# Output projections of a two-block network: modulation folds before additions, norm sums on TensorE alone, a rescale spread over a projection's tiles

## The chip, the cores and the metric

The kernel runs on one core of one Trainium2 chip. The metric is device time in microseconds for one execution of the whole program. Engines are named as the profile names them: PE is TensorE's matmuls and PEld its weight loads, DVE is VectorE, ACT is ScalarE, POOL is GpSimd, SP is SyncE, which issues the DMAs.

## The reference, cut to what matters

Two networks run one after the other on a sequence of 512 tokens with 1024 features. The first has two layers; each ends in an output projection that is added to `x`, and then `x` is normalised. The second opens with a norm whose gain and shift ("modulation") come from a vector `c` times a large weight matrix.

```python
# first block, per layer
h = rms_norm(x, norm_g[layer])
p = h @ w_in[layer]                       # first and second projection
...                                       # attention of two kinds, gated
x = x + mixed @ w_out[layer]              # the output projection "out1"
# after both layers
x = rms_norm(x, final_g)

# second block, per layer l
mod = silu(c) @ ada_w[l, i] + ada_b[l, i] # shift, scale, gate: 3 x 1024 values
h = _rmsnorm(x, norm_g[l, 0]) * (1.0 + scale) + shift
p = h @ ab_w_in[j]                        # the third projection, "pab"
...
x = x + gate * mix
```

All operands are fp32. Products of weights and activations are made in three passes with operands split in a high and a low part: high times high, high times low, low times high.

## The kernel before, in words

Everything is kept transposed: features on the 128 partitions, the 512 tokens along the free axis. `x` is eight tiles (`m.x[:, k]`, KD = 8) of 128 x 512. A "stage" is a block of code for all engines with its own semaphores, closed by a barrier of all engines (L68). Within a stage each engine has its own program in a fixed order written out by hand, and waits for others by semaphore counts; an instruction behind a waiting one on the same engine waits too.

**The output projection of the first block** (`project_out`, stage "out1", once for each layer, so twice) goes over eight output tiles t. For each, SP loads a weight tile of 512 KB into a ring of four slots (`first` and three of `out_raw`), ACT rounds it to its high part (`upper`, L320), DVE makes the low part (`lower`, L327), PE runs 3 x 8 products of 128 x 512 into bank t % 4 (`products_by_half`, L352, L356, L359), and DVE adds the bank to `x` (L1132). Tile t + 4 waits for that addition. `pair`, which holds high and low parts, has two slots. Tile 0's high and low parts of the activations (L1105, L1121) are made beside its products.

Beside it, for the norm of the next stage, `TokenSums` sums the squares of `x` over the features. With a weight it has two chains: squares of x, and squares of x times the gain `final1`. ACT makes both squares of a tile (L138, L140) into two slots `out_sq`. POOL folds them (L150): tiles 1 to 6 are added to an accumulator per chain. At the end PE sums columns (L155): for a chain of 512 tokens it takes four matmuls with 128 x 128 weights and a moving operand of one column of ones, first of the accumulator, then of the last square. Since fp32 matmuls are recorded as two passes, four matmuls show as 8 rows; a tile of both chains is 16 rows. `straight` is the other way of `TokenSums`, used in the opening stage: no accumulator, PE sums the columns of each square, and the slot is free when PE has read it (`freed`); L136 waits for it.

Also beside it, `Modulations` makes one third of a layer's modulation: `c` times a weight matrix that comes in eight chunks of 1024 KB through a ring of four (`ada_ring`, SP, L510). A chunk n of 4 or more waits until chunk n - 4 is folded. DVE folds a pair of chunks in two halves, k = 0 to 3 and 4 to 7 (L528, L531: eight instructions of 128 x 256 a half), with one half in each tile, after the addition of the tile before. `ada_acc` holds two pairs, so pair 2 waits for PE's sum of pair 0, and pair 3 for that of pair 1. PE sums the columns of a pair with four one-column matmuls (L541, 8 rows). `keep` (L549) copies the result out, L1144 and L1146 finish it, and `invert` (L185) turns the root of the token sums into its reciprocal.

SP's order of loads in out1: weights 1 and 2, modulation chunks 0 and 1, weight 3, chunks 2 and 3, weights 4 and 5, chunks 4 and 5, weights 6 and 7, chunks 6 and 7, then the first tile of the next stage's weights.

**The third projection** (`project`, stage "pab", once, behind the second out1) has 35 tiles of 24 products and then four token tiles. It begins with a norm: DVE spreads the reciprocals (L228), PE stretches them over the partitions (L234), DVE and ACT scale, shift, round and split eight tiles (L274, L260, L262, L278) while PE runs the products of tiles 0 and 1 tile by tile of `x` (`first_products`, L292). `TwoNorms` does two norms in one, so `x` itself must still be multiplied by the first norm's gain: `replace` (L1533, eight instructions on `x`), which needs its own `spread.widen` on DVE (L228) and `spread.stretch` on PE (L234, bank 6). It stands on DVE between the norm and the loop over tiles, followed by `bounds.differences` (five tiny operations, L1480 to L1483) and `beside.begin` (L2558, L2559). Then comes the loop: `lower` of tile 2 and so on. `pair` has two slots here, so `upper` of tile 2 waits for the products of tile 0.

Of the kernel before, what the change touches and what calls it, by code (L numbers as in the profile page):

```python
# [28 lines left out]
KD = D // P  # L29
# [41 lines left out]
class Count:  # L71
# [13 lines left out]
    def step(self, ins):  # L85
        self.done(ins)
        self.wait()
# [30 lines left out]
class TokenSums:  # L118
# [34 lines left out]
    def columns(self, pe, what, n, first, last):  # L153
# [3 lines left out]
                                       skip_group_check=True)  # L157
        return mm

    def sum(self, pe):  # L160

        if self.straight:
            for k in range(KD):
                pe.wait_ge(self.squared, k + 1)
                mm = self.columns(pe, self.sq[:, k % 2, 0], 0, k == 0, k == KD - 1)
                mm.then_inc(self.freed if k < KD - 1 else self.summed, 1)
            return
        pe.wait_ge(self.freed, self.chains * (KD - 2))
        for n in range(self.chains):
            self.columns(pe, self.acc[:, n], n, n == 0, False)  # L170
        for n in range(self.chains):
            pe.wait_ge(self.squared, self.chains * (KD - 1) + n + 1)
            mm = self.columns(pe, self.sq[:, (KD - 1) % 2, n], n, False, n == self.chains - 1)
        mm.then_inc(self.summed, 1)
# [872 lines left out]
def project_out(nc, m, name, w, kt, src, gate, follow, down=None, layer=None):  # L1047
# [4 lines left out]
    with stage(nc, name) as sem, ExitStack() as c:  # L1052
# [5 lines left out]
        made, added, rounded, split = sem("made"), sem("added"), sem("rounded"), sem("split")  # L1058
        high, low = sem("high"), sem("low")
        ada = None if layer is None else Modulations(nc, m, c, sem, layer, 2, m.ps[:, 6])  # L1060
        sums = TokenSums(nc, m, c, sem, name, False, None if layer is None else param(m, "final1"))
        following = sem("following")

        with nc.Block(no_gpsimd_drain=True) as block:
            @block.sync
            def _(sp):

                for t in range(KD):
                    ring.load(sp, split, w, t + 1, first=t)
                    if ada is not None and t in (2, 3, 5, 7):  # L1070
                        ada.load(sp, {2: range(2), 3: range(2, 4), 5: range(4, 6), 7: range(6, 8)}[t])

                if follow is not None:
                    if whole:
                        sp.wait_ge(split, 5)
                    sp.dma_start(m.first[:], follow).then_inc(following, 16)
                    sp.wait_ge(following, 16)

            @block.tensor
            def _(pe):  # L1080
                def part(b, k):
                    return parts[:, b, k]

                for t in range(KD):
                    if t >= 4:
                        pe.wait_ge(added, t - 3)
                    first = t == 0 and whole
                    products_by_half(nc, pe, m.ps[:, t % 4], lambda a, k: pair[:, t % 2, a, k], part, kt, t, rounded,
                                     split, high if first else None, low if first else None).then_inc(made, 1)
                    if ada is not None and t in (4, 6):  # L1090
                        ada.sum(pe, t // 2 - 2)
                sums.sum(pe)
                if ada is not None:
                    ada.sum(pe, 2)
                    ada.sum(pe, 3)

            @block.gpsimd
            def _(pool):
                sums.fold(pool)

            @block.scalar
            def _(act):
# [14 lines left out]
            def _(dve):  # L1117
# [7 lines left out]
                for t in range(KD + 1):  # L1125
                    if 1 <= t < KD:
                        lower(nc, dve, ring, pair, rounded, split, t)
                    if t >= 1:
                        j = t - 1
                        dve.wait_ge(made, j + 1)  # L1130
                        if gate is None:
                            ins = nc.vector.tensor_tensor(m.x[:, j], m.ps[:, j % 4], m.x[:, j], ALU.add)  # L1132
                        else:
                            ins = nc.vector.scalar_tensor_tensor(m.x[:, j], m.ps[:, j % 4], gate[:, j:j + 1],  # L1134
                                                                 m.x[:, j], ALU.mult, ALU.add)
                        ins.then_inc(added, 1)
                    if ada is not None and t >= 1:
                        first = (t - 1) % 2 * (KD // 2)
                        ada.fold(dve, (t - 1) // 2, range(first, first + KD // 2))
                if ada is not None:  # L1140
                    ada.keep(dve)
                    flat = m.modf[:].rearrange("p i n -> p (i n)")
# [186 lines left out]
def param(m, name, k=0, n=None):  # L1329
    return param_columns(m.params, name, k, n)  # L1330


def project(nc, m, name, w, norm, places, token_places=(), beside=None, edges=(), tables=(), slots=3, two=None, bounds=None):
# [4 lines left out]
    with stage(nc, name) as sem, ExitStack() as c:  # L1338
# [15 lines left out]
        with nc.Block(no_gpsimd_drain=True) as block:  # L1354
# [13 lines left out]
            @block.tensor  # L1368
            def _(pe):
                def turn(n):  # L1370
                    pe.wait_ge(taken, tiles + n + 1)
                    if n >= 2:
                        pe.wait_ge(placed, n - 1)
                    for i in range(TT):
                        mm = nc.tensor.transpose(m.ps[:, 4 + n % 2, i * P:i * P + P],
                                                 flat[:, n % 2, i * P:i * P + P], m.ident[:])
                    mm.then_inc(turned, 1)

                norm.spread.stretch(pe)
                norm.first_products(pe, (m.ps[:, 0], m.ps[:, 1]), pair, split, made)  # L1380
                if two is not None:
                    two.spread.stretch(pe)
                for t in range(2, total):
                    pe.wait_ge(split, t + 1)
                    if t >= 4:
                        pe.wait_ge(taken, t - 3)
                    products(nc, m.ps[:, t % 4], lambda a, k: pair[:, t % slots, a, k],
                             lambda b, k: norm.to[:, b, k], kt).then_inc(made, 1)
                    if t > tiles:
                        turn(t - 1 - tiles)  # L1390
                if total > tiles:
                    turn(total - 1 - tiles)

            @block.scalar
            def _(act):
# [10 lines left out]
                for t in range(total + 2):  # L1406
                    if slots == 2 and 2 <= t < total:
                        upper(nc, act, ring, pair, rounded, made, t)
                    if bounds is not None and t == 6:
                        bounds.powers(act)  # L1410
                    if 1 <= t <= total:
                        j = t - 1
# [11 lines left out]
            def _(dve):  # L1424
                if two is not None:
                    two.inverse(dve)
                norm.scale(dve, lambda t: lower(nc, dve, ring, pair, rounded, split, t),
                           None if two is None else two.both)
                if two is not None:
                    two.replace(dve)  # L1430
                    bounds.differences(dve)
                dve.wait_ge(zeroed, len(edges))
                if beside is not None:
                    beside.begin(dve)
                for t in range(total):
                    if t >= 2:
                        lower(nc, dve, ring, pair, rounded, split, t)
                    if bounds is not None and t == 8:
                        bounds.values(dve)
                    if beside is not None and t >= 3:  # L1440
                        beside.step(dve, taken, t - 3)
# [54 lines left out]
class TwoNorms:  # L1496
# [28 lines left out]
        self.nc.scalar.activation(self.both[:], self.both[:], ACT.Sqrt, bias=self.m.eps[:, 0:1], scale=1.0 / D)\  # L1525
            .then_inc(self.rooted, 1)

    def replace(self, dve):
        nc, m = self.nc, self.m
        self.spread.widen(dve)  # L1530
        dve.wait_ge(self.spread.stretched, 1)
        for k in range(KD):
            nc.vector.scalar_tensor_tensor(m.x[:, k], m.x[:, k], param(m, "final1", k, 1), m.ps[:, 6],  # L1533
                                           ALU.mult, ALU.mult).then_inc(self.replaced, 1)


def chunk_ends(ap, d):
# [1595 lines left out]
```

## Time and profile before

| | us |
|---|---|
| runs of the kernel before | 2878.0, 2873.0, 2867.95 (median 2873.0) |
| the profiled execution's own time | 2864.47 |
| its span, first to last instruction | 2862.5 |
| PE busy in the span | 2561.8 (89%) |
| DVE / ACT / POOL busy | 1551.0 / 941.7 / 231.6 |
| mean granted TensorE clock | 0.939 of full |
| first out1 stage, first weight issue to L185 | 535.27 to 599.04 |
| second out1 stage, first weight issue to L185 | 1122.15 to 1186.04 |
| third projection, from | 1187.24 |

A row of the timeline reads: start, duration, engine, line, operation, tiles, shape, number of merged instructions, and in brackets how long the engine was idle before it and what ended that. Durations of merged rows reach from the first start to the last end. A granted clock of 1.00 is 2.4 GHz, 0.50 is 1.2 GHz.

### The profile page before, as it was taken

What the parts mean: (1) busy time and instruction counts of PE and PEld (TensorE: products, weight loads), DVE (VectorE), ACT (ScalarE), POOL (GpSimd) and SP (SyncE); (2) the same over time, 40 slices, a digit from 0 to 9 for tenths busy, and PEclk for the clock granted to TensorE, in tenths of its full rate; (3) what the DMA queues carried; (4) which work ended last, traced back from release to release, by engine and by line L of the source; (5) the groups of instructions that cost most, each with busy time, mean ns of one, the idle gap of its engine ahead of it and who ended that gap; (6) DMA issues with size and microseconds to landing.
All of it is one profiled execution on the core that took longest, in us unless ns stands there. A gap on an engine that the chain in (4) does not pass through costs nothing. (4 is left out here: it accounts for less than half of the span.)

```text
span 2862.5 us, 44705 instructions
## 1 busy us (share of the span) xinstructions
PE 2561.8 (89%) x19054; PEld 2062.6 (72%) x19092; DVE 1551.0 (54%) x2240; ACT 941.7 (33%) x1399; POOL 231.6 (8%) x208
## 2 busy tenths in 40 slices
PE   8999899989998999799676988689999896899998
PEld 7888675668886766678564877478878773788877
DVE  3474467863743668725446655654552397445522
ACT  4223124432231245332433333243332322433321
POOL 0000000110000000200152322000001100100011
PEclk9999999989999989799887999799999897999999
DMA  3222223322222133222110000223222121222231
GB/s 134 96 97 96 80 90 124 146 91 96 98 94 84 60 127 134 109 96 96 38 46 15 4 3 4 96 74 103 97 105 109 38 82 44 74 98 94 87 122 50
DMA packets 56106, 238.20 MB, mean 83 GB/s; under 512 B 6560, under 2 KB 7328, under 8 KB 47328
## 3 DMA queue, kind: packets, MB, share of 16 engines
q1 hardware_dynamic: 55904, 235.30, 23.5%
q8 instruction: 153, 2.51, 0.4%
q14 instruction: 49, 0.40, 0.0%
HBM read 231.08 MB, written 4.19 MB: 82 GB/s over the span
## 5 line engine op out<-in xcount | busy, mean ns | idle before, releaser
L341 PE MATMUL banks<-b_h,pin_pair 128*128 128x512 f32 x2304 | 528.3, 390 | 0.0
L341 PEld LDWEIGHTS banks<-b_h,pin_pair 128*128 128x128 f32 x2304 | 431.1, 188 | 88.9
L341 PE MATMUL banks<-ffh,ff_pair 128*128 128x512 f32 x2016 | 457.3, 389 | 0.0
L341 PEld LDWEIGHTS banks<-ffh,ff_pair 128*128 128x128 f32 x2016 | 378.4, 188 | 78.5
L341 PE MATMUL banks<-b_h,pab_pair 128*128 128x512 f32 x792 | 182.4, 392 | 8.0 <-DVE pab_pair L327 8.0
L341 PEld LDWEIGHTS banks<-b_h,pab_pair 128*128 128x128 f32 x792 | 149.9, 190 | 39.4 <-DVE pab_pair L327 8.2
L531 DVE SCALAR_TENSOR_TENSOR ada_acc<-ada_ring,sc,ada_acc 128x256 f32<-128x256 f32 x336 | 158.2, 538 | 0.0
L2680 DVE TENSOR_TENSOR ff<-ff_c,ff 128x512 fp32r<-128x512 f32 x44 | 30.5, 692 | 204.8 <-ACT ff L2668 203.4
L327 DVE TENSOR_TENSOR pin_pair<-pin_raw,pin_pair 128x1024 fp32r<-128x1024 f32 x50 | 61.3, 1226 | 140.1 <-ACT pin_pair L320 140.1
L1134 DVE SCALAR_TENSOR_TENSOR x<-banks,modf,x 128x512 f32<-128x512 f32 x32 | 24.0, 751 | 205.4 <-PE banks L359 205.4
L327 DVE TENSOR_TENSOR pin_pair<-first,pin_pair 128x1024 fp32r<-128x1024 f32 x50 | 61.3, 1226 | 125.3 <-ACT pin_pair L320 125.3
L320 ACT ACTIVATE ff_pair<-ff_raw 128x1024 fp32r<-128x1024 f32 x58 | 61.4, 1059 | 182.4 <-PE banks L341 182.4
L352 PE MATMUL banks<-ff,dn_pair 128*128 128x512 f32 x352 | 87.2, 405 | 13.8 <-ACT dn_pair L320 13.8
L2880 DVE SCALAR_TENSOR_TENSOR cd_acc<-b_hb,params,cd_acc 128x512 f32<-128x512 f32 x120 | 90.2, 752 | 4.0
L320 ACT ACTIVATE dn_pair<-dn_raw 128x2816 fp32r<-128x2816 f32 x16 | 40.9, 2557 | 152.7 <-PE banks L359 142.4
L352 PEld LDWEIGHTS banks<-ff,dn_pair 128*128 128x128 f32 x352 | 69.2, 197 | 29.5 <-ACT dn_pair L320 14.7
L750 ACT ACTIVATE dil_pt<-banks 128x1024 f32<-128x1024 f32 x32 | 32.8, 1025 | 163.1 <-PE banks L676 163.1
L2378 DVE COPY_PREDICATED ru_inv<-rw_levels,banks 128x512 f32<-128x512 uint32 (+1 forms) x80 | 53.7, 677 | 54.1 <-PE banks L2207 54.0
L356 PE MATMUL banks<-ff,dn_pair 128*128 128x512 f32 x352 | 82.4, 389 | 0.0
L359 PE MATMUL banks<-ff,dn_pair 128*128 128x512 f32 x352 | 82.4, 389 | 0.0
L359 PEld LDWEIGHTS banks<-ff,dn_pair 128*128 128x128 f32 x352 | 66.1, 188 | 13.7
L356 PEld LDWEIGHTS banks<-ff,dn_pair 128*128 128x128 f32 x352 | 66.1, 188 | 13.7
(514 smaller groups left out, 4489.9 us busy)
## 6 DMA issues: line engine op xcount, KB each, us to landing
ada_ring<-in_ada_w SPq DMA_DIRECT2D x48, 1024.0 KB, 7.9
ff_raw<-in_ffn_up SPq DMA_DIRECT2D x58, 512.0 KB, 3.7
pin_raw<-in_w_in SPq DMA_DIRECT2D x50, 512.0 KB, 3.5
first<-in_w_in SPq DMA_DIRECT2D x48, 512.0 KB, 3.5
dn_raw<-in_ffn_down SPq DMA_DIRECT2D x16, 1408.0 KB, 6.0
first<-in_ffn_up SPq DMA_DIRECT2D x30, 512.0 KB, 3.5
pab_raw<-in_ab_in SPq DMA_DIRECT2D x23, 512.0 KB, 3.5
out_raw<-in_w_out SPq DMA_DIRECT2D x12, 512.0 KB, 9.0
```

The lines of the kernel that those rows point to most:

```text
L320: nc.scalar.activation(pair[:, t % slots, 0], ring.at(t), ACT.Copy).then_inc(rounded, 1)
L327: nc.vector.tensor_tensor(pair[:, t % slots, 1], ring.at(t), pair[:, t % slots, 0].bitcast(F32), ALU.subtract).then_inc(split, 1)
L341: mm = nc.tensor.matmul(bank, w(a, k), x(b, k), start=k == 0 and i == 0, stop=k == kt - 1 and i == 2)
L352: nc.tensor.matmul(bank, w(0, k), x(0, k), start=k == 0, stop=False)
L356: nc.tensor.matmul(bank, w(0, k), x(1, k), start=False, stop=False)
L359: mm = nc.tensor.matmul(bank, w(1, k), x(0, k), start=False, stop=k == kt - 1)
L531: ins = nc.vector.scalar_tensor_tensor(acc, w, self.m.sc[:, k:k + 1], acc, ALU.mult, ALU.add)
L750: nc.scalar.activation(pt[:, s:s + 2], m.ps[:, s:s + 2], ACT.Exp, scale=scale)\
L1134: ins = nc.vector.scalar_tensor_tensor(m.x[:, j], m.ps[:, j % 4], gate[:, j:j + 1], m.x[:, j], ALU.mult, ALU.add)
L2378: nc.vector.copy_predicated(inv[:, i % 2, f:2, e], over(m.levels[:, d, l, f:2]), m.ps[:, 4 + e, 2 * f * P:].rearrange("p (k t n) -> p k t ...
L2680: chain.step(nc.vector.tensor_tensor(ff[:, 1, j], cv[:, j % 2], ff[:, 0, j].bitcast(F32), ALU.subtract))
L2880: ins = nc.vector.scalar_tensor_tensor(acc[:, k], hb[:, k, tap:tap + T], w[:, 4 * tap + k:4 * tap + k + 1], acc[:, k], ALU.mult, ALU.add)
```

## The change

In `project_out` with a layer (the two out1 stages): the modulation fold of a tile stands on DVE before the addition of the tile before, and one tile earlier (it starts at t = 0); the chunks are asked for earlier; PE sums a modulation pair after tiles 3, 5, 7 instead of 4 and 6 and the end; the token sums go the straight way, with `step` k after tile k + 3, the rest at the end; POOL does nothing. In `project` with two norms (the third projection): the second stretch stands behind tile 3 on PE, its widening in tile 2 on DVE, one of the eight rescales of `x` in each of tiles 6 to 13, `differences` in tile 5, `values` in tile 10 and not 8, and ACT's `powers` in tile 8 and not 6.

```diff
+    def step(self, pe, k):
+        for n in range(self.chains):
+            pe.wait_ge(self.squared, self.chains * k + n + 1)
+            mm = self.columns(pe, self.sq[:, k % 2, n], n, k == 0 and n == 0, k == KD - 1 and n == self.chains - 1)
+        mm.then_inc(self.freed if k < KD - 1 else self.summed, 1)
+
...
-        sums = TokenSums(nc, m, c, sem, name, False, None if layer is None else param(m, "final1"))
+        sums = TokenSums(nc, m, c, sem, name, layer is not None, None if layer is None else param(m, "final1"))
...
                 for t in range(KD):
                     ring.load(sp, split, w, t + 1, first=t)
-                    if ada is not None and t in (2, 3, 5, 7):
-                        ada.load(sp, {2: range(2), 3: range(2, 4), 5: range(4, 6), 7: range(6, 8)}[t])
+                    if ada is not None and t in (1, 2, 3, 5):
+                        n = (1, 2, 3, 5).index(t)
+                        ada.load(sp, range(2 * n, 2 * n + 2))
...
-                    if ada is not None and t in (4, 6):
-                        ada.sum(pe, t // 2 - 2)
-                sums.sum(pe)
-                if ada is not None:
-                    ada.sum(pe, 2)
+                    if ada is not None and t >= 3 and t % 2 == 1:
+                        ada.sum(pe, t // 2 - 1)
+                    if sums.straight and t >= 3:
+                        sums.step(pe, t - 3)
+                if sums.straight:
+                    sums.step(pe, KD - 3)
+                    sums.step(pe, KD - 2)
                     ada.sum(pe, 3)
+                    sums.step(pe, KD - 1)
+                else:
+                    sums.sum(pe)
...
-                sums.fold(pool)
+                if not sums.straight:
+                    sums.fold(pool)
...
                 for t in range(KD + 1):
                     if 1 <= t < KD:
                         lower(nc, dve, ring, pair, rounded, split, t)
+                    if ada is not None and t < KD:
+                        ada.fold(dve, t // 2, range(t % 2 * (KD // 2), t % 2 * (KD // 2) + KD // 2))
                     if t >= 1:
...
-                    if ada is not None and t >= 1:
-                        first = (t - 1) % 2 * (KD // 2)
-                        ada.fold(dve, (t - 1) // 2, range(first, first + KD // 2))
...
                 norm.first_products(pe, (m.ps[:, 0], m.ps[:, 1]), pair, split, made)
-                if two is not None:
-                    two.spread.stretch(pe)
...
+                    if two is not None and t == 3:
+                        two.spread.stretch(pe)
...
-                    if bounds is not None and t == 6:
+                    if bounds is not None and t == 8:
                         bounds.powers(act)
...
-                if two is not None:
-                    two.replace(dve)
-                    bounds.differences(dve)
...
-                    if bounds is not None and t == 8:
+                    if two is not None and t == 2:
+                        two.spread.widen(dve)
+                    if two is not None and 6 <= t < 6 + KD:
+                        two.replace(dve, t - 6)
+                    if bounds is not None and t == 5:
+                        bounds.differences(dve)
+                    if bounds is not None and t == 10:
                         bounds.values(dve)
...
-    def replace(self, dve):
+    def replace(self, dve, k):
         nc, m = self.nc, self.m
-        self.spread.widen(dve)
         dve.wait_ge(self.spread.stretched, 1)
-        for k in range(KD):
-            nc.vector.scalar_tensor_tensor(m.x[:, k], m.x[:, k], param(m, "final1", k, 1), m.ps[:, 6],
-                                           ALU.mult, ALU.mult).then_inc(self.replaced, 1)
+        nc.vector.scalar_tensor_tensor(m.x[:, k], m.x[:, k], param(m, "final1", k, 1), m.ps[:, 6],
+                                       ALU.mult, ALU.mult).then_inc(self.replaced, 1)
```

## Rows read from the trace of the kernel before

**Rows 1.** Page, part 1.

```profile
PE 2561.8 (89%) x19054; PEld 2062.6 (72%) x19092; DVE 1551.0 (54%) x2240; ACT 941.7 (33%) x1399; POOL 231.6 (8%) x208
```

**Rows 2.** Timeline of the first out1, tiles 4 to 7, all engines, cut.

```profile
564.88 5.30 DVE L531 SCALAR_TENSOR_TENSOR ada_acc<-ada_ring,sc,ada_acc 128x256 f32<-128x256 f32 x8
565.70 3.01 POOL L150 TENSOR_TENSOR out_acc<-out_acc,out_sq 128x512 f32<-128x512 f32 x2 [3.95 <-ACT out_sq L138]
566.70 0.95 PE L541 MATMUL banks<-ones,ada_acc 128*128 128x1 f32 x8
567.51 2.11 PE L352 MATMUL banks<-out_parts,out_pair 128*128 128x512 f32 x8
...
577.96 0.68 DVE L1132 TENSOR_TENSOR x<-banks,x 128x512 f32<-128x512 f32 x1
578.09 2.11 PE L359 MATMUL banks<-out_parts,out_pair 128*128 128x512 f32 x8 [0.97 <-DVE out_pair L327]
578.56 3.25 DVE L531 SCALAR_TENSOR_TENSOR ada_acc<-ada_ring,sc,ada_acc 128x256 f32<-128x256 f32 x8
```

**Rows 3.** Timeline of the first out1, its end; the second's is alike, 586.9 later.

```profile
584.62 1.97 PE L359 MATMUL banks<-out_parts,out_pair 128*128 128x512 f32 x8
588.15 2.48 PE L155 MATMUL banks<-ones,out_acc 128*128 128x1 f32 x16 [1.56 <-POOL out_acc L150]
591.28 3.58 PE L155 MATMUL banks<-ones,out_sq 128*128 128x1 f32 x16 [0.65 <-ACT out_sq L138]
...
599.04 0.17 DVE L185 RECIPROCAL rms<-rms 128x4 f32<-128x4 f32 x1
```

**Rows 4.** Stretches: length, PE, PEld, DVE, ACT, POOL busy, PEclk, DMA share, GB/s.

```profile
580.00:586.00 6.00, 6.00 (x32) 5.05 (x31) 6.00 (x10) 1.25 (x2) 6.00 (x3) 1.00 0.00 0
...
588.10:589.40 1.30, 1.25 (x11) 1.25 (x12) 1.30 (x4) 0.00 (x0) 0.00 (x0) 0.99 0.05 13
...
591.30:594.80 3.50, 3.50 (x17) 3.50 (x17) 2.43 (x7) 2.03 (x3) 0.00 (x0) 0.50 0.00 0
...
1877.50:1883.00 5.50, 3.02 (x25) 2.79 (x23) 1.80 (x6) 0.98 (x3) 0.14 (x2) 1.00 0.07 18
...
2846.80:2849.00 2.20, 1.48 (x14) 1.39 (x12) 0.75 (x1) 1.21 (x2) 0.00 (x0) 1.00 0.00 0
```

**Rows 5.** Timeline of the third projection, end of the norm to tile 3.

```profile
1210.91 1.05 PE L234 MATMUL banks<-ident,two_spread 128*128 128x128 f32 x8
1210.92 1.05 ACT L320 ACTIVATE pab_pair<-pab_raw 128x1024 fp32r<-128x1024 f32 x1
...
1218.67 1.23 DVE L327 TENSOR_TENSOR pab_pair<-pab_raw,pab_pair 128x1024 fp32r<-128x1024 f32 x1
...
1219.95 30.41 PE L341 MATMUL banks<-b_h,pab_pair 128*128 128x512 f32 x124 [7.99 <-DVE pab_pair L327]
...
1227.73 0.60 ACT L1417 ACTIVATE hq<-banks 128x512 f32<-128x512 f32 x1 [14.33 <-PE banks L341]
...
1233.17 0.60 ACT L1417 ACTIVATE hq<-banks 128x512 f32<-128x512 f32 x1 [3.89 <-PE banks L341]
```

**Rows 6.** A stretch of the third projection, columns as in rows 4.

```profile
1219.95:1224.20 4.25, 4.25 (x10) 3.38 (x11) 1.08 (x1) 0.00 (x0) 0.00 (x0) 0.50 0.60 213
```

**Rows 7.** Waits, 1187 to 1360: waiter, released by, total us, times, longest.

```profile
DVE pab_pair L327 <- ACT pab_pair L320: 83.0, 26, 8.3
```

**Rows 8.** Loads of the first out1 by window: durations in ns, issue times, landing.

```profile
L510 SPq DMA_DIRECT2D ada_ring<-in_ada_w x2: 333/333/333, 536.3 to 536.8; - x2
DMA to landing us min/median/max: 6.3/7.3/8.3
...
L510 SPq DMA_DIRECT2D ada_ring<-in_ada_w x2: 332/332/333, 556.3 to 556.8; - x2
...
L207 SPq DMA_DIRECT2D out_raw<-in_w_out x1: 1371/1371/1371, 557.3 to 557.3; - x1
DMA to landing us min/median/max: 9.0/9.0/9.0
```

More of the change, by code:

```diff
@@ L163, in sum @@
             for k in range(KD):
-                pe.wait_ge(self.squared, k + 1)
-                mm = self.columns(pe, self.sq[:, k % 2, 0], 0, k == 0, k == KD - 1)
-                mm.then_inc(self.freed if k < KD - 1 else self.summed, 1)
+                self.step(pe, k)
             return
```

## The prediction, made before the changed kernel was run

> **What bounds the kernel now.** I read the page first: PE is busy 89% of 2862.5 us [rows 1], so what the change can win or lose is PE time or PE waits in the three stages that it touches. The chain that ended last covers the final 11 us alone and says nothing of them. So I went to the timeline of each stage. In the first out1, tiles 4 to 7, PE runs product after product; the only stop there that counts is 0.97 us, for the low weights of DVE [rows 2], with a smaller one a tile earlier. A tile of 24 products takes 5.44 us when PE never stops (1227.73 to 1233.17, two evictions [rows 5]); so tile 4 began at 566.70 - 5.44 = 561.26, and to the end of the last product at 586.59 are 25.3 us [rows 2, 3], of which four tiles take 21.8 and two modulation sums 2 x 0.81 = 1.6 (566.70 to 567.51): stops are 1.9. Then comes a tail in which PE waits 1.56 for POOL and 0.65 for ACT [rows 3] and sums columns at half clock [rows 4]; the stage's last DVE operation ends at 599.21 [rows 3]. The second out1 repeats this 586.9 us later. In the third projection PE stands idle 7.99 us while DVE rescales x, [rows 5], and starts tile 2 at half clock [rows 6].
>
> **Part 1, out1: DVE and POOL.** POOL's folds go. A modulation half that ran beside them took 5.30 us, one that ran clear of them 3.25 [rows 2]. DVE per tile is then 1.2 + 3.25 + 0.68 = 5.1 us, below PE's 5.44 and further below what PE gets now. (1.2 for `lower` from [rows 5].) So the 1.9 us of stops and the 1.56 for POOL go. What DVE does earlier costs nothing further: the addition is late by a fold (3.3 us), but tile t + 4 alone waits for it.
> The rule behind the 5.30 is in the Trainium skill (SBUF — State Buffer, "SBUF: two separate sides"): a VectorE operation with two SBUF inputs and a GpSimd operation lock one port pair and the second to come waits out the first. By that rule DVE gains its 2 us a half; it doesn't touch the sum, for PE sets the pace after it.
>
> **Part 2, out1: the start.** The first fold now stands ahead of `lower` of tile 1 and needs chunks 0 and 1, which landed at 536.3 + 6.3 = 542.6 and 536.8 + 8.3 = 545.1 [rows 8], 2.5 apart. They now pass one weight tile, half a chunk, and land 1.25 sooner, at 543.9. Fold 3.25, `lower` 1.2: 548.4. PE needs it for the third pass of tile 1, at 566.70 - 3 x 5.44 - 1.81 = 548.6. It costs 0; if nothing lands sooner, 1.0. Chunks 4 and 5 now stand ahead of weight 4 on SP and wait for the second half fold, which ends near 551.6; where chunks were issued at 556.3 the weight behind them landed at 557.3 + 9.0 = 566.3, 10.0 later [rows 8], so weight 4 lands near 561.7 and is rounded (1.05) by 562.8, ahead of tile 4's new start at 563.9. Nothing is spare there: a chain 2 us later would cost 1 us. ACT's squares now wait for `freed`, with `upper` of the next tile behind them; by the same reckoning that ends 5 us ahead of PE's need for tiles 5 to 7. Modulation pair 3 waits for the sum behind tile 5, near 577; `lower` of tile 7 is done by 583 and needed at 589. All covered, at nothing.
>
> **Part 3, out1: PE.** Here the change adds. The token sums were 16 + 16 one-column rows on PE; straight they are 8 x 16 = 128, and the modulation sums stay at 32. One-column rows at full clock come every 0.112 us (11 in 1.25 [rows 4]); a group of 8 behind products moved the next tile by 0.81 [rows 2], since the first load hides under the last product. From 561.26: 21.8 for the tiles + 160 x 0.112 = 17.9, less 0.4 for the hidden first loads = 600.5 us if the clock holds. Of this 80 rows (8.9 us) are behind the last product, which ends at 591.6.
> The clock: at 589.4, 2.8 us after the last product, the granted clock fell (it was 0.99 over the stretch that ends there), and was 0.50 while PE was busy without a break on one-column rows (17 in 3.50 us, 0.215 apart [rows 4]). At the end of two other output projections it held 5.5 us and 2.2 us past the last product (that ended near 1877.5 and 2846.8) [rows 4]. So it falls 2.2 to 5.5 us behind 591.6; I take the middle, 3.9 to 4.2 behind, 595.8. Left then are 42 rows, at 0.215 in place of 0.112: + 4.3 (early fall + 6.2, late + 3.1). ACT's root and DVE's reciprocal follow the last row at once, + 0.7: 605.5 against 599.2, **+ 6.3 us a stage** (+ 5.1 to + 8.2), **+ 12.6 for both** (10.2 to 16.4). What is late next is therefore PE itself; keep and L1144 are done before.
> The Trainium skill (TensorE: Matmul & The Clock Gate, "Why this matters for your kernels") has the clock drop for want of PE work, and holds it to be enough that no long idle gap comes between bursts of matmuls. The straight sums leave PE no gap, so by that rule it would hold; the rows at 591.30 show a busy PE at 0.50, and I go by them.
>
> **Part 4, third projection.** `lower` of tile 2 needs `upper`, which ends at 1211.97; done then at 1213.25, and PE starts at 1213.3 and not 1219.95: - 6.65 [rows 5]. The 7.9 us gap had brought the clock to 0.50 for 10 products [rows 6], so tile 2 took 1219.95 to 1227.73 = 7.8 us against 5.44 for tile 3 [rows 5]. The new gap is 2.4 us; the stop of 0.97 [rows 2] left the clock at 1.00 [rows 4], the one of 7.99 didn't, and 2.4 is nearer the first: - 2.3 (0 if it falls all the same). The second stretch moves from a gap to behind tile 3, between products: + 1.05 as in its row [rows 5] (2.1 at half clock). Sum **- 7.9** (- 4.6 to - 9, the lowest with the norm's own products at full clock sooner or later by 1). The eight rescales, each like the addition of the same shape, 0.68 [rows 2], go to tiles 6 to 13, where DVE waited for ACT 83 us in 26 tiles, 3.2 a tile [rows 7]; widening, differences, values and powers likewise: 0. If that cover were gone they would cost 8 x 0.68 = 5.4. SP's and POOL's queues aren't touched here.
>
> **Sum.** + 12.6 - 7.9 = + 4.7 us on the profiled execution's 2864.5: 2869.2. That execution is 8.5 below the median of the runs shown; carried to the median of 2873.0 it is **2877.7 us, + 0.16%**. I count 0.3% (8.6 us) as what a measurement of this kernel can tell from no change, so the forecast is: no change that can be told. A measured median can stray by the 5 us that the three runs do.
>
> **Rivals.** (a) *The clock falls between the tiles* (slower). Place: behind tiles 3 and 5 of each stage, where 24 one-column rows in a line, 2.6 us, stand between products, four places in all. Price: what tile 2 of the third projection lost, 2.3 us, for each [rows 5]. It decides from two of the four: + 4.7 + 4.6 = + 9.3; all four give + 14 (2887). For it: one-column rows didn't hold the clock in any tail. Against it: 8 rows between tiles (0.81 us) left it at 1.00 [rows 4], and 2.6 us is near the shortest lag seen, 2.2. 18%.
> (b) *The clock holds through the tail* because PE never idles, the rule named above: + 2.0 a stage (600.5 + 0.7 against 599.2), 4.0 - 7.9 = - 3.9, 2869. Only the tails' late falls speak for it. 10%.
> (c) *One-column rows between tiles cost nothing* since their loads slip under products: then in the tiles 80 rows (8.6 us) a stage vanish, + 6.3 - 8.6 = - 2.3 a stage and - 12.5 in all, 2860: faster. Against: the 0.81 us by which 8 rows moved L352 with PE never idle. 5%.
> (d) *The third projection gives less*: the clock falls in the gap, - 5.6, hence + 7.0 (2880). 9%.
> That the change doesn't do what it says can be left out: the edits are plain orders of work.
>
> **How the numbers follow.** The forecast has 58%. Of it about 4 points lie over + 0.3% (early fall in both stages: 16.4 - 7.9 = + 8.5); (b) lies within; (c) is faster; (a) slower; of (d) 2 points are slower. Faster 0.06, same 0.70, slower 0.24. The range has to hold (b) below (2869, less the scatter of a median) and part of (a) above: 2866 to 2888, which leaves out (c), three or four falls of (a), and odd medians. The likeliest case's own range is 2875 to 2883.
>
> **What would show each step.** POOL without rows in out1; no stop of PE between the tiles, DVE's halves near 3.25 each; groups of 16 and 24 rows L155 and L541 between L359 and L352 that take 1.7 and 2.6 us; about 8.9 us or more of them behind the last L359, with PEclk falling to 0.50 some 4 us into them; 605.5 for the end of the first stage. In the third projection, L341 some 2.4 us behind the last L292 with PEclk 1.00, L234 behind tile 3, L1533 one a tile. The forecast is wrong if PEclk shows 0.50 between out1's tiles, if PE waits for `out_sq` or `out_pair` there, or if the stage ends near 601 or below.

## The result: slower by 0.8%, and the profile after

| | before | after |
|---|---|---|
| median, first comparison (4 and 4 runs) | 2872.52 | 2893.47 |
| ratio, 95% interval | | 1.0083 [1.0064, 1.0101] |
| median, second comparison (11 and 6 runs) | 2868.31 | 2891.14 |
| ratio, 95% interval | | 1.0074 [1.0053, 1.0095] |
| profiled span | 2862.5 | 2889.2 |
| mean granted clock | 0.939 | 0.934 |

The forecast was 2877.7, and the range ended at 2888: the change costs some 21 us, not 5. Every ratio in this document is against runs of the kernel before in the same rounds; their medians were 2867.82 for the first group of experiments below, 2868.59 for the second and 2868.31 for the third. One of the eleven executions of `folds_only` (below) took 4811 us at a mean clock of 0.819, and its ratio leaves that one out.

Part 1 of the page after, to read beside [rows 1]:

```profile
PE 2600.1 (90%) x19246; PEld 2101.3 (73%) x19284; DVE 1528.2 (53%) x2240; ACT 941.9 (33%) x1399; POOL 191.9 (7%) x184
```

PE is busy 38 us longer; DVE gained 23 and POOL 40, which the time does not show. Where it went shows in the stages, each from its first instruction to the first of the next stage, worked out from the timelines (where the next stage first waits some 3 us, its first VectorE instruction is taken). A second profile was taken of either kernel.

| us | before, two profiles | after, two profiles |
|---|---|---|
| first out1 | 68.2, 69.5 | 78.3, 81.1 |
| second out1 | 65.3, 66.1 | 75.3, 75.1 |
| third projection | 218.3, 217.5 | 212.3, 209.2 |
| the three together | 351.7, 353.1 | 365.9, 365.4 |

So the touched stages account for + 13 us, where + 4.7 was forecast. Both out1 stages lose 9 us or more in place of 6.3. The rest of the program, which no edit touches, took 2510.8 and 2514.5 us in the profiles of before, and 2523.3 and 2525.6 in those of after: the change came with some 11 us more there as well.

Timeline of PE in the first out1 after (this stage starts 3.0 us later than before), the places that count, beside [rows 2, 3]:

```profile
564.19 0.95 PE L545 MATMUL banks<-ones,ada_acc 128*128 128x1 f32 x8
565.00 1.93 PE L155 MATMUL banks<-ones,out_sq 128*128 128x1 f32 x16
566.78 2.11 PE L356 MATMUL banks<-out_parts,out_pair 128*128 128x512 f32 x8
...
572.37 1.84 PE L155 MATMUL banks<-ones,out_sq 128*128 128x1 f32 x16
574.07 2.11 PE L356 MATMUL banks<-out_parts,out_pair 128*128 128x512 f32 x8
...
579.65 0.94 PE L545 MATMUL banks<-ones,ada_acc 128*128 128x1 f32 x8
580.46 2.19 PE L155 MATMUL banks<-ones,out_sq 128*128 128x1 f32 x16
582.51 3.41 PE L356 MATMUL banks<-out_parts,out_pair 128*128 128x512 f32 x8
...
594.88 1.98 PE L363 MATMUL banks<-out_parts,out_pair 128*128 128x512 f32 x8
596.70 0.94 PE L545 MATMUL banks<-ones,ada_acc 128*128 128x1 f32 x8
597.50 8.98 PE L155 MATMUL banks<-ones,out_sq 128*128 128x1 f32 x48
606.35 1.84 PE L545 MATMUL banks<-ones,ada_acc 128*128 128x1 f32 x8
608.05 3.55 PE L155 MATMUL banks<-ones,out_sq 128*128 128x1 f32 x16
611.94 0.18 DVE L189 RECIPROCAL rms<-rms 128x4 f32<-128x4 f32 x1 [2.89 <-ACT rms L184]
```

No row of PE in this stretch has an idle time in brackets: the stops of [rows 2] are gone. 24 one-column rows move the next tile by 2.59 us (564.19 to 566.78), 16 by 1.70 (572.37 to 574.07). But the first eight products behind tile 5's 24 rows took 3.41 us in place of 2.11. The stretches of the same trace, columns as in [rows 4], show the clock there:

```profile
574.10:581.90 7.80, 7.80 (x46) 6.80 (x47) 2.53 (x6) 2.19 (x3) 0.00 (x0) 1.00 0.00 1
582.10:585.30 3.20, 3.20 (x10) 2.62 (x11) 2.56 (x7) 2.19 (x3) 0.00 (x0) 0.50 0.03 5
585.50:596.70 11.20, 11.20 (x59) 9.48 (x58) 4.55 (x10) 1.24 (x2) 0.00 (x0) 1.00 0.00 0
596.70:599.00 2.30, 2.30 (x23) 2.30 (x21) 0.69 (x1) 0.00 (x0) 0.00 (x0) 1.00 0.00 0
599.20:611.60 12.40, 12.40 (x59) 12.32 (x58) 0.62 (x3) 3.97 (x6) 0.00 (x0) 0.50 0.00 0
1182.80:1186.10 3.30, 3.30 (x10) 2.62 (x10) 2.85 (x6) 2.19 (x3) 0.00 (x0) 0.50 0.02 5
1240.90:1244.10 3.20, 3.20 (x9) 2.52 (x8) 0.93 (x1) 0.00 (x0) 0.00 (x0) 0.50 0.80 215
```

The clock fell from 1.00 (2.4 GHz) to 0.50 (1.2 GHz) in the midst of PE's work, at the end of tile 5's 24 one-column rows, in either out1; it fell again some 2.4 us behind the last product, and then 59 rows took 12.40 us, 0.21 apart. Behind tile 3, where 24 rows stand in a line too, it held. The last row is the third projection's tile 2: there it fell as well. Timeline of that place after, beside [rows 5]:

```profile
1224.33 13.35 PE L296 MATMUL banks<-b_h,pab_pair 128*128 128x512 f32 x45 [0.69 <-DVE pab_pair L331]
...
1238.69 1.23 DVE L331 TENSOR_TENSOR pab_pair<-pab_raw,pab_pair 128x1024 fp32r<-128x1024 f32 x1 [5.46 <-ACT pab_pair L324]
...
1239.97 12.81 PE L345 MATMUL banks<-b_h,pab_pair 128*128 128x512 f32 x48 [2.28 <-DVE pab_pair L331]
...
1247.38 0.60 ACT L1427 ACTIVATE hq<-banks 128x512 f32<-128x512 f32 x1 [7.36 <-PE banks L345]
...
1252.62 1.05 PE L238 MATMUL banks<-ident,two_spread 128*128 128x128 f32 x8
1252.82 0.60 ACT L1427 ACTIVATE hq<-banks 128x512 f32<-128x512 f32 x1 [3.89 <-PE banks L345]
...
1259.18 0.60 ACT L1427 ACTIVATE hf<-banks 128x512 f32<-128x512 f32 x1 [3.52 <-PE banks L345]
...
1261.98 0.74 DVE L1544 SCALAR_TENSOR_TENSOR x<-x,params,banks 128x512 f32<-128x512 f32 x1
...
1264.62 0.60 ACT L1427 ACTIVATE hf<-banks 128x512 f32<-128x512 f32 x1 [3.89 <-PE banks L345]
```

The wait shrank from 7.99 to 2.28 us; tile 2 still took 7.41 (1239.97 to 1247.38), tile 3 the full-speed 5.44.

### The profile page after: what moved, and what is told of

It reads as the page before. It is cut to its first block and busy times, and to the rows that moved or that the text cites. A ratio compares the mean times of both kernels' runs of the same rounds, so it can differ in the third digit from the quotient of the medians.

```text
span 2889.2 us, 45043 instructions
## 1 busy us (share of the span) xinstructions
PE 2600.1 (90%) x19246; PEld 2101.3 (73%) x19284; DVE 1528.2 (53%) x2240; ACT 941.9 (33%) x1399; POOL 191.9 (7%) x184
## 5 line engine op out<-in xcount | busy, mean ns | idle before, releaser
L345 PEld LDWEIGHTS banks<-ffh,ff_pair 128*128 128x128 f32 x2016 | 378.4, 188 | 78.5
L535 DVE SCALAR_TENSOR_TENSOR ada_acc<-ada_ring,sc,ada_acc 128x256 f32<-128x256 f32 x336 | 137.6, 477 | 0.0
L356 PE MATMUL banks<-ff,dn_pair 128*128 128x512 f32 x352 | 87.3, 405 | 13.8 <-ACT dn_pair L324 13.8
L356 PEld LDWEIGHTS banks<-ff,dn_pair 128*128 128x128 f32 x352 | 69.3, 198 | 29.6 <-ACT dn_pair L324 14.7
L360 PEld LDWEIGHTS banks<-ff,dn_pair 128*128 128x128 f32 x352 | 66.1, 188 | 13.7
L363 PEld LDWEIGHTS banks<-ff,dn_pair 128*128 128x128 f32 x352 | 66.1, 188 | 13.7
```

The source lines that it names most:

```text
L345: mm = nc.tensor.matmul(bank, w(a, k), x(b, k), start=k == 0 and i == 0, stop=k == kt - 1 and i == 2)
L356: nc.tensor.matmul(bank, w(0, k), x(0, k), start=k == 0, stop=False)
L360: nc.tensor.matmul(bank, w(0, k), x(1, k), start=False, stop=False)
L363: mm = nc.tensor.matmul(bank, w(1, k), x(0, k), start=False, stop=k == kt - 1)
L535: ins = nc.vector.scalar_tensor_tensor(acc, w, self.m.sc[:, k:k + 1], acc, ALU.mult, ALU.add)
```

## The experiments

The touched stages of each run stand against the mean of the two profiles of before (68.8, 65.7, 217.9; together 352.4).

**The parts alone, and before once more.** `again_before` is the kernel before. `pab_only` is before with the third projection's edit alone. `folds_only` has the change's order of folds, loads and modulation sums, with POOL's accumulator kept. `straight_only` has the straight token sums with the old order of folds and loads. Neither touches the third projection. Lines with a minus are those of the kernel after.

```diff
  folds_only
-        sums = TokenSums(nc, m, c, sem, name, layer is not None, None if layer is None else param(m, "final1"))
+        sums = TokenSums(nc, m, c, sem, name, False, None if layer is None else param(m, "final1"))
...
  straight_only
-                    if ada is not None and t >= 3 and t % 2 == 1:
-                        ada.sum(pe, t // 2 - 1)
+                    if ada is not None and t in (4, 6):
+                        ada.sum(pe, t // 2 - 2)
                     if sums.straight and t >= 3:
                         sums.step(pe, t - 3)
```

> The kernel before once more, for a second profile. If what the trace of after lost outside the three changed stages (about 12 of 26 us) is chance of the clock's falls, this profile lies near 2870 and not 2862, and its untouched stages differ from the first profile's by several us in the same places (around 340, 930 and 1660 us). If they are a consequence of the change, this profile repeats the first within 1 us outside the out1 stages.

> Only the third projection's part (rescales among the tiles). My theory: tile 2 starts 6.6 us sooner, the stretch costs 1, and the clock falls in the gap as it did in the trace of after: - 6 us, ratio 0.998. Rival (the rescales or the later powers hold something up): 0 or slower. Out1 stages as before: 64 us each from the first weight issue to the reciprocal.

> Only the token sums by PE alone in out1, with the old order of folds, loads and modulation sums. If one-column rows on PE and the half clock behind them are the cost, each out1 stage is 8 to 10 us longer than before, + 16 to + 20 in all, ratio 1.006 to 1.007. If the new order of folds and loads is the cost, it is within 2 us a stage.

> Only the folds and loads ahead and the modulation sums behind tiles 3, 5 and 7, with POOL's folds of the squares kept. If PE's rows are the cost: within 2 us a stage of before (DVE and POOL still hold each other up, and the last addition comes 1 to 2 us later, the modulation sums 2 sooner), ratio 0.998 to 1.002. If the order is the cost: + 8 to + 10 a stage.

| | median | ratio | first, second out1 | third projection |
|---|---|---|---|---|
| again_before | 2870.39 (one run) | | 69.5, 66.1 | 217.5 |
| pab_only | 2862.74 | 0.9985 [0.9972, 0.9997] | 69.5, 66.2 | 211.8 |
| straight_only | 2895.51 | 1.0105 [1.0085, 1.0125] | 79.0, 75.8 | 217.9 |
| folds_only | 2877.12 | 1.0031 [1.0016, 1.0046] | 74.2, 71.5 | 218.4 |

The third projection's edit gains 6.1 us in its stage. The straight sums alone cost 10.1 us a stage, the whole loss of out1: the new order of folds gives next to nothing back (9.5 in the first profile after). The ratio of `straight_only` is above the 1.006 to 1.007 expected, for its median holds 7 us more than its stages. And that order alone loses 5.6 us a stage, where at most 2 was expected and none of my terms had a loss. Its timeline at the end of the first out1:

```profile
589.25 2.96 POOL L150 TENSOR_TENSOR out_acc<-out_acc,out_sq 128x512 f32<-128x512 f32 x2 [3.87 <-ACT out_sq L138]
589.57 5.31 DVE L535 SCALAR_TENSOR_TENSOR ada_acc<-ada_ring,sc,ada_acc 128x256 f32<-128x256 f32 x8
...
594.80 1.27 DVE L1147 TENSOR_TENSOR x<-banks,x 128x512 f32<-128x512 f32 x2
...
596.22 2.49 POOL L150 TENSOR_TENSOR out_acc<-out_acc,out_sq 128x512 f32<-128x512 f32 x2 [4.00 <-ACT out_sq L138]
...
598.76 3.57 PE L155 MATMUL banks<-ones,out_acc 128*128 128x1 f32 x16 [6.16 <-POOL out_acc L150]
```

The last fold, slowed by POOL to 5.31 us, now stands ahead of the additions of tiles 6 and 7, which come together at 594.80; ACT's squares, POOL's fold and PE's sums follow in a chain, and PE waits 6.16 us for POOL in place of 1.56 [rows 3]. So folds ahead of additions are harmless only once POOL's folds are gone: the two edits depend on each other. (The order of loads moved with them and was not tested by itself; PE's longer wait is 4.6 of the 5.6 us.)

In `straight_only` the 24 rows stand behind tiles 4 and 6, for the modulation sums are still there, and its stretches have the falls there, two a stage:

```profile
581.50:584.70 3.20, 3.20 (x9) 2.52 (x8) 1.41 (x2) 1.13 (x2) 0.00 (x0) 0.50 0.18 72
598.60:601.80 3.20, 3.20 (x9) 2.52 (x8) 0.16 (x1) 0.16 (x1) 0.00 (x0) 0.50 0.00 0
1175.50:1178.70 3.20, 3.20 (x9) 2.46 (x8) 1.46 (x2) 1.19 (x2) 0.00 (x0) 0.50 0.22 90
1192.60:1195.70 3.10, 3.10 (x9) 2.40 (x8) 0.20 (x1) 0.20 (x1) 0.00 (x0) 0.50 0.00 0
```

**The rows moved, made fewer, and added.** `split_rows` is after with each token step ahead of its tile's third pass, so that 16 and 8 rows no longer stand in a line. `two_columns` is after with one square for both chains: x² stays the stationary operand, and the moving one gets two columns, ones and the gain's square. `rows_tail` is before with 48 rows (24 matmuls whose result nobody reads) behind the token sums. `best` is `two_columns` with step t - 2 behind tile t, the last steps between the passes of tile 7, the modulation sums behind tiles 3, 5 and 6 and inside tile 7, and 8 rows left behind the last product.

```diff
  split_rows, in products_by_half
+    if between is not None:
+        between()
     pe.wait_ge(split, t + 1)
...
  two_columns, in TokenSums
+    def weigh(self, pool):
+        self.nc.gpsimd.memset(self.by[:, 0], 1.0).then_inc(self.weighted, 1)
+        self.nc.gpsimd.tensor_tensor(self.by[:, 1], self.weight, self.weight, ALU.mult).then_inc(self.weighted, 1)
...
+            for i in range(TT):
+                mm = self.nc.tensor.matmul(self.m.ps[:, 7, 0:2 * TT].rearrange("p (n i) -> p n i", n=2)[:, :, i],
+                                           self.sq[:, k % 2, 0, i * P:i * P + P], self.by[:, :, k],
...
  rows_tail
                 sums.sum(pe)
                 if ada is not None:
+                    for i in range(24):
+                        nc.tensor.matmul(m.ps[:, 5, i:i + 1], sums.acc[:, 0, i % 4 * P:i % 4 * P + P],
+                                         m.ones[:, 0:1], start=i == 0, stop=i == 23, skip_group_check=True)
...
  best
-                    if sums.straight and t >= 3:
-                        sums.step(pe, t - 3)
+                    if sums.straight and 2 <= t < KD - 1:
+                        sums.step(pe, t - 2)
```

> The changed kernel with the token sums of tile t - 3 ahead of the third pass of tile t instead of behind it, so that never more than 16 one-column rows stand in a line between tiles (24 behind tiles 3, 5, 7 in the changed kernel). The number of rows is the same. If the clock's fall between the tiles comes from 24 rows in a line, it goes, and each out1 stage is 2 us shorter (77 to 75), - 4 us in all. If any 16 rows do it: no difference, falls still there.

> The changed kernel, but one square per tile and a moving operand of two columns (ones and the squared gain), so that a tile's token sums are 8 rows of PE and not 16, and ACT makes one square. The sums are the same ones. If PE's rows are the cost: 64 rows fewer a stage, 32 between tiles at 0.112 us and 32 in the tail at up to 0.215, with the falls between tiles gone: - 9 to - 12 us a stage, 2870 or somewhat less in all. If the cost was in the order of DVE, ACT and SP: at most 2 us a stage.

> The kernel before with 48 additional one-column rows behind the token sums, into an unused bank (they compute nothing that is used). They stand in the part at half clock: 48 x 0.2135 = 10.3 us a stage, + 20.5 in all, if a longer stage costs its own length. If a later start of what follows costs something too (the changed kernel and the one with the straight sums alone lost 5 to 11 us more in the medians than their out1 stages show), it is + 26 to + 31.

> Two columns as in two_columns; besides, token sums of tile t - 2 behind tile t, the last two and the last modulation sum inside tile 7 ahead of its second and third pass, so that only 8 rows are left behind the last product. By PE's count: 21.8 us for tiles 4 to 7 and 88 rows at 0.112, then addition, square, 8 rows and root 3.6 us: a stage 3 us shorter than before (64 against 67.5), with the third projection's 6: 2855, ratio 0.995 to 0.996. If rows inside a tile bring the clock down: 2 us a stage less gain.

| | median | ratio | first, second out1 | third projection |
|---|---|---|---|---|
| split_rows | 2882.16 | 1.0048 [1.0029, 1.0066] | 75.6, 72.3 | 212.1 |
| two_columns | 2858.87 | 0.9971 [0.9957, 0.9985] | 64.6, 61.6 | 209.2 |
| rows_tail | 2892.12 | 1.0080 [1.0059, 1.0100] | 79.6, 76.4 | 217.6 |
| best | 2852.45 | 0.9944 [0.9925, 0.9964] | 66.0, 62.6 | 211.8 |

In `split_rows` the clock nowhere falls between the tiles, and the stages are 2.7 and 3.0 us shorter than in the first profile after, with the same 160 rows. By the price worked out below, one fall is some 1.7 of that; the other us is put down to the tail, for 16 rows of tile 7 now lie ahead of the last product's end. One stretch of it, and PE's timeline around one such group:

```profile
560.00:597.00 37.00, 37.00 (x204) 31.91 (x204) 28.24 (x60) 12.07 (x17) 0.00 (x0) 1.00 0.46 183
```

```profile
582.58 1.84 PE L155 MATMUL banks<-ones,out_sq 128*128 128x1 f32 x16
584.28 2.11 PE L365 MATMUL banks<-out_parts,out_pair 128*128 128x512 f32 x8
586.23 0.95 PE L547 MATMUL banks<-ones,ada_acc 128*128 128x1 f32 x8
587.03 2.09 PE L356 MATMUL banks<-out_parts,out_pair 128*128 128x512 f32 x8
```

That bears out rival (a): with the rows apart the falls between tiles are gone, the number of rows being the same.

`rows_tail` isolates the price of the tail. Its 48 rows in the first out1:

```profile
603.45 10.38 PE L1095 MATMUL banks<-ones,out_acc 128*128 128x1 f32 x48
```

0.216 us each, half clock from first to last, and either stage is 10.7 us longer. The medians say + 23.5 where the stages say + 21.1: what such a stage loses arrives in the total nearly one for one.

`two_columns` halves the token rows. Its rows in PE's timeline, behind tile 6 and behind the last product:

```profile
590.40 0.95 PE L174 MATMUL banks<-out_by,out_sq 128*128 128x2 f32 x8
...
597.55 2.87 PE L174 MATMUL banks<-out_by,out_sq 128*128 128x2 f32 x24
600.28 1.07 PE L564 MATMUL banks<-ones,ada_acc 128*128 128x1 f32 x8
601.21 1.85 PE L174 MATMUL banks<-out_by,out_sq 128*128 128x2 f32 x8
```

Eight rows of two columns between products take 0.95 us, as eight of one do; 24 in the tail take 2.87. The second chain is free on PE, and ACT makes one square a tile and not two. The stages are 13.7 us shorter than after and 4 us shorter than before. `best` has only eight token rows behind the last product, at full clock, and waits 1.44 us for the square of tile 7:

```profile
600.48 2.11 PE L386 MATMUL banks<-out_parts,out_pair 128*128 128x512 f32 x8
604.04 1.05 PE L174 MATMUL banks<-out_by,out_sq 128*128 128x2 f32 x8 [1.44 <-ACT out_sq L142]
```

By stages `best` is 1.4 and 1.0 us behind `two_columns` in out1; by the medians it is 6 us faster. It has the lowest median of all, and both beat the kernel before. The profiled execution of `best` was its slowest (2863.49 against a median of 2852.45), so its stages need not be those of the median; which of the two is better is left open, for their intervals overlap.

**After once more, and out1's part alone.** `again_after` is the changed kernel; `out_only` is after with the old third projection.

```diff
  out_only, in project
+                if two is not None:
+                    two.replace(dve)
+                    bounds.differences(dve)
                 dve.wait_ge(zeroed, len(edges))
```

> The changed kernel itself, once more, timed in the same rounds as the kernel before and with a second profile. The sum over the three touched stages is +18.7 for out1 and -6.0 for the third projection, +12.7 us, while the medians differ by 21 to 25 us and the first profile of the kernel before lay 8.5 us below its median. Theory 'only the touched stages differ, the rest of the gap is scatter of single profiles and of medians': the three stages repeat within 0.5 us (78.3, 75.3, 212.3), the falls between tiles come back at the same two places, the untouched stages come out nearer those of before, and the median ratio is near +12.7/2868, 1.0045 to 1.006. Rival 'a longer or different stage also costs something further on': the ratio repeats 1.008 and untouched stages hold 5 us or more again.

> The whole change in the two output projections, with the third projection left as it was. By the stages it costs 9.3 us in each out1, +18.7, ratio 1.0065; against again_after it differs by the third projection's 6 us. Theory 'parts add': out_only minus again_after is 4 to 8 us in the medians. Rival 'parts do not add' (the third projection's gain depends on the clock that the out1 tail leaves, or the out1 loss is larger in medians than in stages): a difference under 2 or over 10 us, or a ratio over 1.009.

| | median | ratio | first, second out1 | third projection |
|---|---|---|---|---|
| again_after | 2891.14 | 1.0074 [1.0053, 1.0095] | 81.1, 75.1 | 209.2 |
| out_only | 2895.74 | 1.0102 [1.0081, 1.0122] | 78.5, 75.1 | 217.8 |

The parts add: `out_only` less `again_after` is 4.6 us in the medians, and `pab_only` gained 5.1. Two other expectations missed. If only the touched stages differed, the ratios had to be 1.0045 to 1.006 and near 1.0065; they are 1.0074 and 1.0102, so what the unchanged code lost came back. And the falls did not come back at the same two places. Stretches of `again_after`:

```profile
573.60:576.90 3.30, 3.30 (x10) 2.53 (x9) 3.30 (x7) 1.73 (x3) 0.00 (x0) 0.50 0.99 390
590.70:594.00 3.30, 3.30 (x9) 2.53 (x9) 2.92 (x6) 1.67 (x3) 0.00 (x0) 0.50 0.00 0
...
1191.50:1194.60 3.10, 3.10 (x9) 2.42 (x9) 2.69 (x6) 2.19 (x3) 0.00 (x0) 0.50 0.02 5
```

The clock fell at three of the four places with 24 rows this time, at two in the first profile and at two in `out_only`; with `straight_only`'s four it is 11 of 16, and none with 16 rows. Taken by place, there is more of a pattern. Tile 3's 24 rows, with no token rows ahead of them, saw it fall in 1 of 6 stages; the 24 rows with 16 token rows one tile ahead (tile 5 in these kernels, tiles 4 and 6 in `straight_only`) in 10 of 10. The fall came 2.3 to 3.9 us after the first of the 24 rows. So both the length of the line (`split_rows`) and the rows of the tile ahead go with the fall; no run varies the latter by itself. In the third projection the clock this time held through the same wait:

```profile
1246.77 10.50 PE L345 MATMUL banks<-b_h,pab_pair 128*128 128x512 f32 x45 [2.28 <-DVE pab_pair L331]
...
1252.55 0.60 ACT L1427 ACTIVATE hq<-banks 128x512 f32<-128x512 f32 x1 [5.73 <-PE banks L345]
```

Tile 2 took 5.78 us, and the stage is 8.7 us shorter than before instead of 5.6. At this place, as at tile 3, whether the clock falls is thus not fixed by the kernel's text; it differs between executions.

## Why the prediction was wrong

The sum of the touched stages was forecast at + 4.7 us and came out at + 13.4 and + 13.0; the medians differ by 21 and 22.8. Two steps failed: the clock between the tiles (with the tail's fall and the third projection's gain mis-sized beside it), and the silent one that the rest of the program keeps its time. For the first profile the pieces nearly close the first gap: falls between tiles 2 x 1.7, tails 2 x 1.7, the third projection's clock 2.3, together 9.1 against 8.7.

- **Part 1 held.** POOL has no row in out1, DVE's halves take 3.25, PE never stops for DVE. The Trainium skill (SBUF — State Buffer, "SBUF: two separate sides") has a two-input VectorE operation and GpSimd's shut each other out; the 5.31 us of `folds_only` with POOL beside it and the 3.25 after agree. What I did not see is that the order of folds is safe only with POOL's folds gone.
- **Part 2 held.** Tile 4's products were forecast to start at 563.9 and start at 566.78 less the 3.0 by which the stage is late: 563.8.
- **Part 3, the price of a row, held**, and so did "late next is PE itself". The sums at full clock cost 0.11 us a row, in the tail at half clock 0.21.
- **Part 3, the clock between the tiles: this step failed.** I took rival (a) for unlikely (18%), because 8 rows had left the clock at 1.00 and 2.6 us was "near the shortest lag seen, 2.2". It fell in two and three of the four places, in every profile behind tile 5. Each costs about 1.7 us: the 3.41 for L356 is 1.3 over, the rows ahead of it 0.4. `split_rows` shows by taking the line apart that the line of 24 matters; that the rows of the tile ahead go with it too is seen only by comparing places. The rival's price (2.3) was somewhat high and its chance too small. The 8 rows that had kept the clock said nothing of 24, and the lag of 2.2 us had been seen behind a last product, so 2.6 us of rows was already longer than it.
- **Part 3, the tail: mis-sized.** The fall came 2.3 and 2.5 us behind the last product in the two stages, not 4.05; in `again_after` 3.2 and 2.6. That makes the first stage's 80 rows 14.9 us (596.70 to 611.60) against 13.2. The lags lie within the 2.2 to 5.5 of the prediction; its middle was too late. In `straight_only` the lags were 4.3 and 4.2.
- **Rival (b) is refuted.** The Trainium skill (TensorE: Matmul & The Clock Gate, "Why this matters for your kernels") has it that the clock holds if no long idle gap comes between bursts. Here PE was busy 7.80 of 7.80 us and then ran at 0.50. The measurement decides: one-column fp32 products are work to the profile's busy column and did not keep the clock there. Rival (c) is refuted too: 24 rows moved a tile by 2.59 us.
- **Part 4, the order of events, held**: PE starts tile 2 at 1239.97, which is 1213.4 on the clock of before (its L292 and after's L296 are 26.6 us apart); forecast 1213.3. The second stretch behind tile 3 moved the next eviction by 0.9 (1252.82 to 1259.18 is 6.36 against 5.44), forecast 1.05. The rescales cost nothing: one a tile, evictions 5.44 apart. The gain of 2.3 by the clock came in one profile of after and failed in the other. Of the six profiles with the short wait the clock fell in four (the first of after, `pab_only`, `split_rows`, `best`) and held in two: rival (d)'s 9% was too little.
- **The unchanged code: this step failed as well, and its cause stays open.** The sum was carried to the median as if the rest of the program kept its time, and the prediction gave no reason for it. Medians differ by 8 to 10 us more than the touched stages. `out_only`, `straight_only` and `two_columns` have 7 to 8 us more too, `split_rows` 6; `best`, `pab_only` and `folds_only` have none (- 4 to 0), `rows_tail` 2. In the profiles part of it lies between the two out1 stages: 518.7 and 514.3 us before, 522.1 and 522.8 after, at a mean clock of 0.95 and 0.96 against 0.94 and 0.94, and 521.2 to 522.5 in `split_rows`, `two_columns` and `best`; but 518.6 in `out_only` and 515.2 in `straight_only`. Such stages also vary for themselves: the attention stage ahead of the first out1, ahead of every edit, took 115.1 us in the first profiles of before and after and 121.1 to 121.3 in the other kernels', with some 12.7 and 29 us of it at 0.50. Chance alone is unlikely, for the second profiles and medians repeated the loss; by what way the edits would shift the clock elsewhere, no run here shows. Without it the median would stand at 2873.0 + 13.4 = 2886.4, inside the range by 2 us; that would have been luck, for the + 4.7 that the forecast rested on had failed.

## What to carry to other kernels

Before an accumulator is taken from an idle engine and its sum given to the one that sets the pace, price the rows at both clocks and see how many stand in a line: 96 rows more a stage cost 10 us net here, and what they replaced had kept PE waiting only 3.5. Column sums by a one-column product cost about what their weight loads do (PEld was busy for 2.30 of the 2.30 us from 596.70, and a second column was free), so put every chain of sums that shares the stationary operand into one product as further columns (- 13.7 us a stage against after), and place the groups between passes of wide products rather than in a tail. Test edits that look independent one by one: the new order of folds, loads and modulation sums cost 5.6 us a stage with POOL's folds, and nothing without.

## What was not expected of the hardware

- PE busy without a gap does not keep the clock: at 24 one-column fp32 rows in a line (2.6 us) it fell to 0.50 in 11 of 16 places and stayed there for some 3.3 us, most of it wide products; at 16 rows (1.8 us) in none. With 16 token rows one tile ahead it was 10 of 10, with none ahead 1 of 6.
- A 128x2 fp32 moving operand costs PE what a 128x1 does, 0.95 us for eight rows behind products. The Trainium skill (TensorE: Matmul & The Clock Gate, "LDWEIGHTS (loading the stationary operand)") gives a load its columns over 1.2 in ns; by it an estimate for 128 columns is 107 ns, near the 0.11 us of a row at 2.4 GHz. At 1.2 GHz the rows were 0.21 apart.
- The same instructions meet another clock from one execution to the next: the third projection's tile 2 took 7.41 us in one profile of after and 5.78 in the other, behind an equal wait of 2.28.
